# Recurrence of a hybrid block: where the second direction's Gram products stand in TensorE's order of work

## The reference, cut to what matters

```python
def step(state, inp):
    r_t, w_t, k_t, v_t, kk_t, kka_t = inp
    sa = jnp.einsum('bhvk,bhk->bhv', state, kk_t)
    state = state * w_t[:, :, None, :] - sa[..., None] * kka_t[:, :, None, :] + v_t[..., None] * k_t[:, :, None, :]
    return state, jnp.einsum('bhvk,bhk->bhv', state, r_t)
y_f, s_fwd = wkv7_scan(s0_fwd, rh, dec_f, k_f, vh, kk, kk * a_f, reverse=False)
y_b, s_bwd = wkv7_scan(s0_bwd, rh, dec_b, k_b, vh, kk, kk * a_b, reverse=True)
```

## Time and profile before

| | |
|---|---|
| median of three runs | 3932.25 us (3930.14 to 3936.12) |
| the profiled execution, its own time | 3928.69 us |
| its span in the trace | 3926.9 us |
| TensorE busy over the span | 90% |
| mean granted TensorE clock | 0.98 |
| stage of the recurrence (turns 0 to 15) | from 194.75 us to about 1400 us |
| one turn in the middle of the stage | about 74 us |

### The profile page before, as it was taken

The page is one execution under the profiler, slowest core; times in us unless marked ns, Lnnn a source line. Parts: engine busy times, 40 slices in busy tenths (PEclk is TensorE's granted clock), DMA queues, the critical chain, the costliest instruction groups (busy, mean ns, idle before and its releaser), DMA issues. The chain is left out here.

```text
span 3926.9 us, 72072 instructions
## 1 busy us (share of the span) xinstructions
PE 3530.5 (90%) x30735; PEld 2121.6 (54%) x30735; DVE 1864.1 (47%) x3194; ACT 683.9 (17%) x1242; POOL 1133.0 (29%) x1734
## 2 busy tenths in 40 slices
PE   7999999999999789999999999989877777777776
PEld 3456666666666546666688888475332323333332
DVE  1334544544544448877830000156465565564644
ACT  2223223223223112122210000011110110100101
POOL 2044344334335201001000000024444444444442
PEclk9999999999999889999999999999999999999998
DMA  9322222222222157776753435359999999999997
GB/s 381 111 70 76 62 71 73 64 71 71 66 71 66 48 166 247 223 254 200 231 191 141 171 129 207 125 236 427 395 427 428 428 427 428 428 427 428 428 427 311
DMA packets 473389, 906.04 MB, mean 231 GB/s; under 512 B 85180, under 2 KB 307086, under 8 KB 403854
## 3 DMA queue, kind: packets, MB, share of 16 engines
q0 software_dynamic: 73728, 536.90, 32.5%
q1 hardware_dynamic: 307664, 318.46, 24.6%
q10 hardware_dynamic: 91710, 46.43, 4.0%
HBM read 889.04 MB, written 12.68 MB: 230 GB/s over the span
## 5 line engine op out<-in xcount | busy, mean ns | idle before, releaser
L2558 PE MATMUL ps<-w_slots,diag 128*128 128x512 f32 x1920 | 899.4, 615 | 257.9 <-DMA w_slots<-in_peer_v,ixv 224.6
L2558 PEld LDWEIGHTS ps<-w_slots,diag 128*128 128x128 f32 x1920 | 356.8, 194 | 798.5 <-issue 465.8
L994 PE MATMUL ps<-hT,w_slots 128*128 128x512 f32 (+1 forms) x1536 | 617.8, 536 | 4.2 <-PEq L230 2.2
L1684 PE MATMUL ps<-hT,w_slots 128*128 128x256 f32 (+1 forms) x1504 | 497.5, 487 | 6.9 <-PEq L655 4.9
L2171 POOL DMA_INDIRECT w_slots<-in_peer_v,ixv x244 | 264.6, 1084 | 596.8 <-PE ps L2558 513.5
L2335 DVE SCALAR_TENSOR_TENSOR junk<-w_slots,hT 128x2048 f32<-128x2048 f32 x128 | 293.5, 2293 | 271.2 <-DMA w_slots<-in_peer_u,ixu 267.2
L2335 DVE SCALAR_TENSOR_TENSOR junk<-ybT,hT 128x2048 f32<-128x2048 f32 x128 | 293.4, 2292 | 263.5 <-DMA ybT<-in_peer_u,ixu 263.0
L1684 PEld LDWEIGHTS ps<-hT,w_slots 128*128 128x128 f32 x1504 | 284.1, 191 | 180.2 <-issue 159.3
L994 PEld LDWEIGHTS ps<-hT,w_slots 128*128 128x128 f32 x1536 | 270.7, 189 | 169.7 <-issue 144.9
L724 POOL TENSOR_TENSOR Ypart<-Ym,Sm 128x126 f32<-128x126 f32 (+22 forms) x496 | 190.3, 384 | 491.5 <-DMA Sm<-s_blocks 453.9
L2428 ACT ACTIVATE diag<-ident,coef 128x128 f32<-128x128 f32 x240 | 94.6, 401 | 904.6 <-PE ps L2558 892.4
(11 more groups left out here) (382 smaller groups left out, 4378.2 us busy)
## 6 DMA issues: line engine op xcount, KB each, us to landing
w_slots<-in_w_mod SPq DMA_DIRECT2D x128, 512.0 KB, 5.7
w_slots<-in_w_in SPq DMA_DIRECT2D x56, 1024.0 KB, 6.1
w_slots<-in_w_in ACTq DMA_DIRECT2D x44, 1024.0 KB, 7.7
w_mod_ring<-in_w_mod SPq DMA_DIRECT2D x16, 2048.0 KB, 13.6
w_slots<-in_w_in SPq DMA_DIRECT2D x7, 4096.0 KB, 13.9
w_slots<-in_w_branch_a SPq DMA_DIRECT2D x4, 4096.0 KB, 14.0
w_slots<-in_w_branch_b SPq DMA_DIRECT2D x4, 4096.0 KB, 13.8
w_slots<-in_w_out SPq DMA_DIRECT2D x4, 4096.0 KB, 12.7
```

Source lines behind the costliest of these rows:

```text
L994: last = mm(ps[:, 4, t0:TOK], w[m % 2][:, k, :], hT[:, k, t0:TOK], start=(k == 0), stop=(k == KC - 1))
L1684: last = mm(out, w[m % SLOTS_W][:, k, :], hT[:, k, t0:TOK], start=(k == 0), stop=(k == KC - 1))
L2558: last = nc.tensor.matmul(ps[:, 4 * n + c, :], diag[:, k % 2, :], vb[k % NB][:, c * 512:(c + 1) * 512], start=False, stop=False)
```

## The change

`gram(1, 0, i)` and `gram(1, 1, i)` come directly behind `gram(0, 0, i)` and `gram(0, 1, i)`, ahead of `piece("k", 0, 2)` and `chain(1, z)`. All other engines' orders stay as they are.

```diff
@@ -1175,11 +1175,11 @@
                     if B:
                         gram(0, 0, i)
                         gram(0, 1, i)
+                    if B:
+                        gram(1, 0, i)
+                        gram(1, 1, i)
                     piece("k", 0, 2)
                     chain(1, z)
-                    if B:
-                        gram(1, 0, i)
-                        gram(1, 1, i)
                     piece("k", 2, 4)
                     chain(2, z)
                     if B:
```

More of the change, by code:

```diff
@@ L1177, in _ @@
                         gram(0, 1, i)
-                    piece("k", 0, 2)
-                    chain(1, z)
                     if B:
@@ L1182, in _ @@
                         gram(1, 1, i)
+                    piece("k", 0, 2)
+                    chain(1, z)
                     piece("k", 2, 4)
```

## The result

The change made the kernel slower. Five executions took 3960.74 to 3977.14 us, median 3968.12; the kernel before took 3932.25. The ratio is 1.0095, 95% interval 1.0082 to 1.0108. In a second series the same change gave 3974.4 against 3932.64 us, ratio 1.0112 (1.0097 to 1.0126). I had forecast 3958 us and a range of 3946 to 3969. The sign and the holes came as forecast; the cost was 36 us (in the second series 42) in place of 26, at the very edge of the range or past it.

A forecast was written before the change was run, and what follows sets the result against it. TensorE's own stream was taken to set the pace. Terms 22.2 + 1.0 - 0.6 + 0.8 + 0 + 2.6 = 26 us raised the profiled 3928.69 to 3954.7; as a median, 3958 us, range 3946 to 3969.

The forecast's parts named there:

- Part 2: Second Gram products: 256 instructions last 1.33 us, the next block needs 3.4, so an unhidden 2.1 us hole in nearly every turn.
- the eleven usual turns: Turns 2 to 7, 9, 10, 12, 13, 14: 11 x 2.1 us of holes, less present ones, 22.2 us.
- Part 3: In turns 1, 8 and 11 the next block is fetched early: hole 0.6 us; turn 8 net -0.6 us.
- the bold 3.4 us: TensorE's instruction blocks of 256 cannot begin closer together than about 1.1 + 2.3 = 3.4 us.
- Part 4: `masked(1)` and the path through `solved` about 0.45 us later; only turns 1 and 11 pay, 1.0 and 0.8 us with holes.
- Part 5: Turn 0: `g1` stays, key steps end 1.9 us later, the 6.84 us wait swallows this; net 0.
- Part 6: Turn 15: `masked(1)` and the 11.59 us wait for `solved` end 2.6 us later.
- A: Rival: blocks are there in time, only the order counts; net -1 us or -6, 3926 to 3931 us; chance 0.07.
- B: Rival: fetches begin sooner, holes only 0.6 to 1.1 us; 15 us in all, 3943 to 3950 us; chance 0.13.
- C: Rival: longer holes of 3.1 us, or `solved` waits in more turns; 43 us, up to 3975 us; chance 0.10.
- D: Rival: only the path through `solved` pays, at most 0.45 x 15 = 7 us; 3933 to 3939 us; chance 0.04.

The follow-up runs named there:

- The two grids: Two kernels with the changed order and repeated small products, the block grid lying elsewhere in each: near grid 4012.83 us, far one 4044.65 us.
- The long and the short wait of the experiments: Kernel before plus a TensorE wait each turn behind the second Gram products, for VectorE's gi1 (long, 3968.88 us) or st (short, 3950.19 us).
- the spread value steps: Kernel before with value steps 6 to 8 ahead of additions(0), and 9 and 10 between additions(0) and additions(1): 3924.01 us against 3931.4, ratio 0.9982.
- the near grid: Changed order with one small product repeated 23 and 22 times in turns 1 to 14, boundary about 17 instructions behind Gram products' start: 4012.83 us.
- the far one: The near grid kernel with 36 more repeats in turn 0 alone, boundary about 130 instructions behind the Gram products' start: 4044.65 us.

## Why the prediction was right and where it failed

*Part 2, the block grid: right.* The hole in the eleven usual turns was 2.05 us on the mean (1.58 to 2.49), forecast 2.1, and blocks began 3.1 to 4.0 us apart. The two grids show it as the cause, not only as what the trace suggests. The grid itself is stricter than I had seen: counted with the sequencer's own instructions, all 22 idle times named "issue" of over 0.25 us in the stage before, and all 38 after, end at the same place of the grid of 256. The statement of the Trainium skill ("Runtime: NRT & Kernel Launch", "Instruction fetch mechanics") that refills are hidden fails in this kernel wherever two blocks are wanted sooner than that.

*Part 3, the three turns with an early fetch: right.* Holes of 0.30, 0.49 and 0.71 us, forecast 0.6; turn 8 got shorter, by 0.7. There two blocks begin only 1.8 to 2.2 us apart, so the bold 3.4 us of the prediction holds only where the fetch starts behind the boundary.

*Part 2, "Nothing hides it" and a hole priced as its length: this is the step that failed.* A hole has a second price. Behind it the clock may be half for a stretch, in which the two key steps take 3.4 us in place of 2.0. In the six turns of the eleven that have half clock the way from the first key matmul to the ninth took 8.7 to 9.1 us in place of 7.4, 9.5 us in all. (These turns paid 3.84 - 1.88 = 1.96 us each more than the five others, but 0.3 of that is longer holes.) The eleven usual turns came out 10.2 us above their 22.2, so this is nearly all that the forecast missed there. The sum had no term for it, though the earlier trace rows stood at 0.99 and not at 1.00, and half-clock stretches around the long waits of turns 0 and 15 were to be seen in the trace before. The long and the short wait of the experiments show the term by itself: 28.7 us of waits cost 38 us, 19.1 us cost 19.

In the second profile of the changed kernel the term is smaller: four of the eleven turns have half clock, 6.1 us, and the eleven are 9.5 us above the forecast. Some 2 us of that are longer holes at L1126 and L1130 than in the first profile; the rest is open.

*Part 4, the path through `solved`: right in kind, small.* In turn 2 `masked(1)` began 0.4 us behind the first of the chain's two instructions. The kernel that moves the products past the chain step only prices the whole path at 3 us or less. The +1.0 us for turn 1 did not come: `masked(1)` was 0.9 us later there, but the way from sending `St` to reading it back took 2.4 us in place of 3.8, and the wait of 0.87 us was gone. Of the eleven profiled executions only two have that wait (the kernel before, and the one past the chain step with 0.69 us), and I had treated it as a property of the turn.

*Part 5, turn 0: nearly right.* `masked(1)` came 0.3 us earlier in the turn and not 1.9, nearly as argued; the wait fell to 3.20 us, not to about 5, since it swallowed the slow key steps too. The turn got 0.5 us shorter.

*Part 6, turn 15: 5.2 us in place of 2.6.* The hole in its first Gram products grew from 1.97 to 3.06 us, where I had left it as it was, and the projection steps behind ran at half clock (3.49 us).

*The total* of 3958 us was saved by luck from being further off: turn 1 came out 1.9 us and turns 0, 8 and 11 together 1.0 us under their terms, against 10.2 us above in the usual turns and 2.6 in turn 15.

*The rivals.* A needed the next block to be fetched ahead of the boundary; it was so in three turns only. B's holes of 0.6 to 1.1 us stayed to those turns. C came near the total by the wrong term: it made the hole longer, and it was the clock. D's path costs 3 us at most by the kernel past the chain step.

## What to carry to other kernels

Count TensorE's instructions, not only its time: where small matmuls run faster than 256 instructions in 3.4 us, put long matmuls between them, as the spread value steps did here. Read idle time named "issue" as a late block when it recurs every 256 instructions. An order that looks free, since it moves no work and breaks no dependence, can take away that cover. In this kernel a standstill of about 2 us on TensorE cost its own length and, in about half the cases, 1.6 us more.

## What the runs showed that I had not expected

The granted clock was at half behind holes of only 1.9 to 2.4 us in a stage where TensorE is otherwise busy nearly all the time. In one kernel it also fell without any hole: in eight turns of the near grid, right behind 23 repeats of one small product, in a stretch where TensorE was never idle for over 0.06 us. The Trainium skill, "TensorE: Matmul & The Clock Gate", Part 1, says that the clock follows how busy the array has been; the repeated products agree with that better than with idle time alone. They don't settle it: the same repeats were followed by half clock in 8 of 14 turns of the near grid and in 1 of 14 of the far one. Which holes are followed by it stays open: turn 9 of the changed kernel had the longest usual hole, 2.49 us, and kept its clock, and of fifteen waits of the same length in one kernel eight were followed by it and seven not.
